# Low parts of twelve weight pieces from accumulating DMAs in place of VectorE subtractions

## The reference

```python
hdn = rms_norm(x, norm_w[layer]) * (1.0 + scale[:, None, :]) + shift[:, None, :]
q1, k1, v1, g1, q2, k2, v2, g2 = jnp.split(hdn @ w_in[layer], 8, axis=-1)
...
y = jnp.concatenate([y1 * jax.nn.silu(g1), y2 * jax.nn.silu(g2)], axis=-1) @ w_out[layer]
x = x + gate[:, None, :] * y
```

## Time and profile before

| | us |
|---|---|
| median of 3 timed runs | 352.9 |
| lowest and highest | 351.12, 353.72 |
| profiled execution, its own time | 348.91 |
| span of the profiled execution | 347.1 |

### The profile page before, as it was taken

One profiled execution on the slowest core, in us unless ns is written; L12 is line 12 of the kernel. 1 busy time (PEld: TensorE's weight loads), 2 busy tenths in 40 slices (PEclk: granted clock), 3 DMA queues, 4 the chain that ended last, 5 costly groups with the idle time before them and its releaser, 6 DMA issues.

```text
span 347.1 us, 4880 instructions
## 1 busy us (share of the span) xinstructions
PE 294.3 (85%) x1733; PEld 244.3 (70%) x1733; DVE 251.3 (72%) x495; ACT 209.1 (60%) x414; POOL 13.6 (4%) x20
## 2 busy tenths in 40 slices
PE   2289888997888979769689599999999879998795
PEld 2168766776667868568478488889888669887584
DVE  2898889788788598697978747758674744785633
ACT  3545468556664878889256445666655675998300
POOL 0000000000002732000000000000000000000000
PEclk9999999999899999989999989999999999999999
DMA  7999999565556366369556805457557446210011
GB/s 258 370 413 354 374 354 384 183 246 212 187 209 242 124 236 249 127 241 361 203 160 180 294 12 174 139 180 237 184 199 237 147 152 217 78 62 0 0 62 60
DMA packets 19879, 70.31 MB, mean 203 GB/s; under 512 B 2192, under 2 KB 2576, under 8 KB 19856
## 3 DMA queue, kind: packets, MB, share of 16 engines
q1 hardware_dynamic: 19856, 70.01, 56.6%
HBM read 68.95 MB, written 1.05 MB: 202 GB/s over the span
## 4 chain that ended last, share of the span: by engine, by line
PE 44%; DVE 28%; ACT 18%; issue 7%; DMA 2%; SPq 0%; ACTq 0%; DVEq 0%
PE proj L984 29%; DVE w_lo L677 8%; PE score L984 8%; DVE raw L693 7%; ACT w_hi L409 4%; PE mixed L984 3%; ACT probs L510 2%; DMA xs<-in_x 2%; PE turned L1029 1%; ACT gt L556 1%; PE turned L1011 1%; DVE y L862 1%; DVE gt L854 1%; DVE n_ms L811 1%; DVE hy_lo L865 1%
## 5 line engine op out<-in xcount | busy, mean ns | idle before, releaser
L677 DVE TENSOR_TENSOR w_lo<-raw,w_hi 128x1024 fp32r<-128x1024 f32 x80 | 97.4, 1228 | 20.2 <-ACT w_hi L409 19.8
L409 ACT ACTIVATE w_hi<-raw 128x1024 fp32r<-128x1024 f32 x80 | 82.7, 1049 | 13.3 <-DMA raw<-in_w 12.2
L984 PE MATMUL proj<-w_hi,hy_hi 128*128 128x512 f32 x176 | 74.1, 421 | 12.8 <-DVE hy_lo L725 7.7
L984 PE MATMUL proj<-w_lo,hy_hi 128*128 128x512 f32 x176 | 70.5, 400 | 0.0
L984 PE MATMUL proj<-w_hi,hy_lo 128*128 128x512 f32 x176 | 70.4, 400 | 0.0
L693 DVE CUSTOM_DVE_ANT_0 raw<-raw,c_rows 128x1024 f32<-128x1024 f32 x48 | 58.8, 1245 | 0.0
L984 PE MATMUL proj<-hy_hi,w_hi 128*128 128x256 f32 x192 | 57.4, 299 | 0.0
L984 PE MATMUL proj<-hy_lo,w_hi 128*128 128x256 f32 x192 | 54.8, 285 | 0.0
L984 PE MATMUL proj<-hy_hi,w_lo 128*128 128x256 f32 x192 | 54.7, 285 | 0.0
L984 PEld LDWEIGHTS proj<-w_hi,hy_hi 128*128 128x128 f32 x176 | 34.3, 195 | 22.7 <-DVE hy_lo L865 6.8
L984 PEld LDWEIGHTS proj<-w_hi,hy_lo 128*128 128x128 f32 x176 | 34.1, 193 | 7.8
(11 more groups left out here) (139 smaller groups left out, 374.3 us busy)
## 6 DMA issues: line engine op xcount, KB each, us to landing
raw<-in_w SPq DMA_DIRECT2D x80, 512.0 KB, 4.1
raw<-in_w_mod SPq DMA_DIRECT2D x48, 512.0 KB, 5.0
xs<-in_x SPq DMA_DIRECT2D x1, 1024.0 KB, 5.8
out_x<-xs SPq DMA_DIRECT2D x4, 256.0 KB, 2.0
cst<-in_constants SPq DMA_DIRECT2D x1, 520.0 KB, 6.3
logits<-in_a_lambda SPq DMA_DIRECT2D x1, 128.0 KB, 12.5
rows<-in_vectors SPq DMA_DIRECT2D x1, 64.0 KB, 1.9
cst<-in_constants SPq DMA_DIRECT2D x1, 64.0 KB, 2.0
```

Source lines behind the costliest of these rows:

```text
L409: nc.scalar.activation(w_hi[:, n % PIECES, :, :], raw_tile(("w", n)), ACT.Copy).then_inc(hi_done, 1)
L677: nc.vector.tensor_tensor(w_lo[:, n % PIECES, :, :], raw_tile(("w", n)), w_hi[:, n % PIECES, :, :], ALU.subtract).then_inc(lo_done, 1)
L984: return nc.tensor.matmul(o, a, b, start=start, stop=stop, skip_group_check=True)
```

## The change

For the twelve even pieces n from 12 to 34 (`by_dma`), ScalarE makes a second copy behind `w_hi`: `w_lo = -round(raw)`, an activation of the same kind with scale -1. GpSimd then issues a DMA that adds `raw` to `w_lo` in place, float32, which leaves raw - round(raw), the same low part. VectorE's `split_lo` of these pieces goes. TensorE waits for the DMA's semaphore before the first use of the piece, and SP waits for it before it loads the slot of `raw` anew. GpSimd issues the DMAs of pieces 12 to 22 ahead of its wait for the Q2 tile, those of 24, 26, 28 and 30 between the bias maps (24 ahead of map 8, 26 ahead of map 10, 28 ahead of map 12, 30 ahead of map 14), and those of 32 and 34 at the end.

```diff
+def by_dma(n):
+    return 12 <= n < 36 and n % 2 == 0
+def lows(n):
+    return sum(by_dma(i) == by_dma(n) for i in range(n + 1))
...
+        def wait_lo(eng, n):
+            if by_dma(n):
+                eng.wait_ge(lo_dma[n % PIECES], 16 * sum(by_dma(i) for i in range(n % PIECES, n + 1, PIECES)))
+            else:
+                eng.wait_ge(lo_done, lows(n))
...
                     else:
-                        sp.wait_ge(lo_done, was[1] + 1)
+                        wait_lo(sp, was[1])
...
                 nc.scalar.activation(w_hi[:, n % PIECES, :, :], raw_tile(("w", n)), ACT.Copy).then_inc(hi_done, 1)
+                if by_dma(n):
+                    nc.scalar.activation(w_lo[:, n % PIECES, :, :], raw_tile(("w", n)), ACT.Copy,
+                                         scale=-1.0).then_inc(neg_ok, 1)
...
                     for n in pieces_lo(layer, g):
-                        if n >= 12:
+                        if n >= 12 and not by_dma(n):
                             split_lo(n)
...
+            def add_raw(n):
+                pool.wait_ge(neg_ok, lows(n))
+                nc.gpsimd.dma_start(w_lo[:, n % PIECES, :, :].bitcast(F32), raw_tile(("w", n)),
+                                    accum_op=ALU.add).then_inc(lo_dma[n % PIECES], 16)
+
             pool.wait_ge(cst_in, 16)
+            pieces = [n for n in range(PIECES_OF) if by_dma(n)]
+            for n in pieces:
+                if FIRST[n] <= 46:
+                    add_raw(n)
             wait_turned(pool, ("qk", 0, Q2, 1))
             for M in range(8, 16):
+                for n in pieces:
+                    if 46 < FIRST[n] and FIRST[n] // 2 - 24 == M - 8:
+                        add_raw(n)
...
+            for n in pieces:
+                if FIRST[n] >= 64:
+                    add_raw(n)
...
                 if at == FIRST[n]:
-                    pe.wait_ge(lo_done, n + 1)
+                    wait_lo(pe, n)
```

## The result

The changed kernel takes 364.8 us (median of 4 runs, 362.1 to 365.4) against 352.4 of before, timed beside it: 12.5 us slower in the medians, where 3.6 were forecast; it lies outside the predicted range. The ratio of the two is 1.034, with a 95% interval of 1.028 to 1.039.

What follows compares the result with a forecast made beforehand. At each even piece (50 to 152 us) it asked which engine the next step awaited, VectorE, ScalarE or TensorE; 0.9 - 0.5 - 0.1 + 1.9 + 1.05 + 0.35 = +3.6 us on 352.9 gave 356.5, range 350.0 to 362.0.

Steps and rivals of the forecast that it cites:

- terms 1 to 3 and 5: Pieces 12 to 16 +0.9 us; 18 and 20 -0.1 and -0.5; 22 and 24 +0.95 each; 32 and 34 +0.35.
- the exchange at piece 20: VectorE's normalising no longer waits behind its own subtraction but for ScalarE's exponential, delayed 0.95 us by the negation: -0.5 us.
- Term 4: Piece 24's DMA, issued late by GpSimd, delays the load of piece 28, for which ScalarE waits: +1.05 us.
- L: Time from GpSimd's turn to the landing of piece 24's adding DMA: 6.8 us, between 3.1 and 13.
- Other covers: Low parts of the other pieces land before TensorE needs them; slot loads about 5 us later stay hidden by the ring.
- The covers of TensorE's own waits: Time from a low part's issue to TensorE's first use: 8 us at piece 12, 12 at 14, similar or more later.
- Rival (a): The adding DMA is quick, L below 4.5 us, so piece 28 isn't late: +1.9, 354.8 us; chance 0.22.
- (b): The adding DMA is slow, L about 12.3 us, and TensorE stalls openly on piece 24: 362.0 us; chance 0.13.
- (c): Full DMA engines before 61 us delay the adds of 12 and 14 and `w_hi` 17: 359.5 us; chance 0.08.
- (d): VectorE alone sets the pace of 50 to 145 us; six removed `w_lo` save 6.8 us: 346.1 us; chance 0.10.

Runs made afterwards that it cites:

- x2_neg_only: The changed kernel without its twelve DMAs, ScalarE's negations kept (low parts wrong): 355.0 us against 350.7 for the kernel before, ratio 1.011.

## Why the prediction was wrong

**The sign and terms 1 to 3 and 5.** They can be held against x2_neg_only, which has just these. The forecast drift at step 28 was +0.9, the profile has +1.0; at step 36, after pieces 18 and 20, +0.3 against +0.4; after 22 and 24 +2.2 against +2.8 to +3.6; from there to step 54, with no load late, -0.65 against -0.8. Summed, +1.9 was forecast, and the profile has +2.9 at step 80, the timed runs 3.8 by their ratio. The step-by-step reading of ScalarE's order was right in kind and 2 us low; an estimate from the clocks in the last section puts most of these 2 us down to the lower granted clock, for which the sum had no term. In the changed kernel the exchange at piece 20 is as described: `w_hi`, negation, exponential, with VectorE now 0.89 us idle for it.

```profile
81.56 1.05 ACT L426 ACTIVATE w_hi<-raw 128x1024 fp32r<-128x1024 f32 x1
82.51 1.05 ACT L428 ACTIVATE w_lo<-raw 128x1024 fp32r<-128x1024 f32 x1
83.46 0.39 ACT L530 ACTIVATE probs<-logits,stat 128x128 f32<-128x128 f32 x1
...
84.46 0.17 DVE L811 RECIPROCAL stat<-stat 128x2 f32<-128x2 f32 x1 [0.89 <-ACT probs L530]
```

**Term 4, mis-sized: the load behind the add.** The place was right: GpSimd's turn comes late, SP's load into piece 24's slot was issued at 121.20 (117 plus the drift was forecast, and the drift came to 5.6), and `w_hi` 28 waited. L was guessed at 6.8 us and was shorter here, 4.5, about the value under which the prediction had said that piece 28 isn't late. But the load of piece 28 was taken at 4.0 us, the median of a kernel in which loads go out two by two; it took 7.7. With 4.0 it would have landed at 125.6, and ScalarE was ready for it at 125.85: the whole wait of 3.47 us is the slow load. SP had a row of loads to issue at once, and the add of piece 26 ran beside them. From step 50 to step 54 the lag grew by 3.6 us (by 4.5 up to step 52) where 1.05 stood; putting the add early gave back 3.2 by the ratios.

**"Other covers" is the step that failed.** The prediction said that loads into an even piece's slot come about 5 us later, "hidden as long as the ring of seven holds it ahead of its use", and gave this cover no size. The rows for a size were there. In the kernel before, around pieces 18 and 22:

```profile
71.67 1.23 DVE L677 TENSOR_TENSOR w_lo<-raw,w_hi 128x1024 fp32r<-128x1024 f32 x1 [0.79 <-ACT w_hi L409]
...
78.06 0.33 SPq L380 DMA_DIRECT2D raw<-in_w  x1
...
89.93 1.04 ACT L409 ACTIVATE w_hi<-raw 128x1024 fp32r<-128x1024 f32 x1
```

Piece 18's slot came free at 72.9 us. Piece 22's load, which stands behind the load into that slot, was issued at 78.06 and landed 3.1 us later, and `w_hi` 22 began at 89.93: 5.2 us were free ahead of the load and 8.7 behind it, 13.9 in all. In the changed kernel the slot was held for 9.5 us longer after `w_hi` 18 (the negation, 0.3 us of wait and an add of 9.5, where `w_lo` had needed 1.25), the load was issued 0.4 us behind the landing, and it took 8.0 us in place of 3.1, 4.9 more. That is 14.8 or so against 13.9, and `w_hi` 22 waited, 1.4 us when the small drifts are counted in. With an add of 6.8 us, or with a load of 4.0, it would not have waited. At piece 32 the hold alone was too long: 1.9 and 3.5 us were free before and behind the load of piece 37, the slot was held for 6.1 us longer, and the load took 1.3 us more. So two things failed: the load of 4.0 us, which the prediction used and the runs contradict with 7.7 and 8.0, and the cover, which was called enough without a number. In the table of lags the places other than piece 24 come to 4.4 us.

The covers of TensorE's own waits, which had been worked out, held: in 45 to 185 us TensorE waited for no low part.

**L.** The bounds, 3.1 to 13, held the twelve landings of 4.5 to 10.5, and the median of 7.2 is near the 6.8 worked out from the load of 1024 KB. What failed is that one value was used for piece 24 alone, whereas a dozen adds, some of them of 9.5 to 10.5 us, work on one ring. Rival (a) came near in L for piece 24, 4.54 us, and the time was lost all the same, to the load. The formula that the prediction cites for it (the Trainium skill, DMA: Bandwidth & Descriptors, Anatomy of one DMA — SWDGE (gpsimd) path), by which 3.2 or 4.4 us were estimated, doesn't hold for these adds beside loads: the fastest took 4.54, the others 5.5 to 10.5.

**Rivals.** (b), a slow DMA, came nearest in time (362.0) and named the wrong wait: TensorE on piece 24. Its sign, a landing over 9 us, came three times (pieces 18, 22 and 30), without a wait of TensorE. (c) was right that the adds of 12 and 14 are slow (7.3 and 6.0 us), but `w_hi` 17 began at 67.37, three us after its load had landed, and no wait for them shows. (d) was right on what relieving VectorE is worth (6.8 forecast for six subtractions, 7.7 measured without all twelve) and wrong that ScalarE would have room; the rows said so.

**The range** reached to 362.0 and was missed by 2.8 us, as neither the slower loads nor the covers without a size had a share in it.

**What stays open.** The 0.3 to 0.6% between the negations alone and the versions with DMAs in which the hold, the bytes or the adding is gone are within the intervals; no run settles what they are. How the 12 us divide between the waits themselves and the lower clock behind them is only estimated, in the last section; no run holds the clock fixed. What inside the DMA system slows a load beside an add isn't shown either. A ring of eight slots would have been the obvious control; no run has it.

## What to carry to other kernels

When a change makes the freeing of a buffer wait for something longer, write down for each buffer the time from its release to the use of what is loaded next, and of what is loaded behind it, less that load's own time; that is the cover, and it goes to the add, to the load behind it in the queue's order, and to the slowing of loads that go out together. Before handing work from one engine to another, look whether the receiving engine has a gap between two things that the giving engine waits for: here both were on the chain in turn, and 7.7 us of relief cost 11 us of new work. And time a candidate more than once, and compare the granted clocks: one execution of the copying kernel was 5 us under its median.

## What the runs showed of the hardware

An adding DMA of 512 KB within SBUF, issued by GpSimd beside loads, takes 4.5 to 10.5 us to land, a copying one 2.9 to 9.9, an add of 64 KB 2.3 to 8.4; GpSimd's issue of one lasts 0.85 to 1.0 us for an add of either size and 0.53 to 0.67 for a copy. Loads of 512 KB that pile up behind a held slot beside such adds go from 4.1 us in the median to 8.4 (84 to 104 us).

A subtraction of 1024 columns on GpSimd (2.4 to 3.3 us) makes a two-column operation of VectorE last 1.8 us in place of 0.22; cut in four, 0.5.

The granted clock of TensorE, in one stretch: in the changed kernel TensorE had waited 2.36 us at 58.97 for `qn`, and from 60.5 us on the clock was at its lower level (1.2 GHz), where a matmul took 0.63 in place of 0.39 us. In the kernel before it had waited 1.73 us at the same place and the clock stayed at 2.4 GHz. The views by stretch (us, busy time of each engine, then the granted clock, DMA share and GB/s), first before, then after:

```profile
60.50:64.00 3.50, 3.28 (x19) 2.49 (x18) 2.97 (x8) 3.21 (x7) 0.00 (x0) 1.00 0.57 177
```

```profile
60.50:63.50 3.00, 3.00 (x11) 2.42 (x10) 2.50 (x7) 2.13 (x7) 0.00 (x0) 0.50 0.97 280
```

TensorE's wait in the kernel before, then its wait and one of the longer matmuls in the changed kernel:

```profile
58.44 0.66 PE L1011 MATMUL turned<-cst,qn 128*128 128x128 f32 x4 [1.73 <-DVE qn L837]
```

```profile
58.97 0.66 PE L1047 MATMUL turned<-cst,qn 128*128 128x128 f32 x4 [2.36 <-DVE qn L857]
...
62.95 0.63 PE L1020 MATMUL proj<-w_hi,hy_lo 128*128 128x512 f32 x1
```

What the mean clock of an execution goes with shows best in one kernel. The kernel before was timed beside each experiment; its eleven runs with a mean clock of 0.985 took 348.7 us on the mean, its nine with 0.966 took 352.5: 4 us for 0.019. The mean over all its runs was 0.977, that of the changed kernel's 0.956 (0.948 to 0.967). An estimate from these: some 4 of the 12 us go with the lower clock. At the same clock the changed kernel took 362.1 us (its one run with 0.967) against the 352.5, 9.6 us more. The kernel with the negations alone had 0.969, 1.7 us by the same reckoning, of its 3.8. The mean clock is lower than 0.977 in each of the timed kernels here that are slower than the one before, so this may be a part of what each wait costs rather than a cause beside it; no run separates the two. Single profiles of one kernel differ with it too: the copying kernel took 352.3 us at 0.985 and 356.5 at 0.971.
